# Sum of squares of the context norm: three additions on GpSimd and one product with ones, in place of eight products

## The reference

```
def rms_norm_2(x, w):
    x32 = x.astype(jnp.float32)
    y = x32 * lax.rsqrt(jnp.mean(x32 * x32, axis=-1, keepdims=True) + EPS)
    return (y * w.astype(jnp.float32)).astype(x.dtype)
...
    hc = modulate(rms_norm_2(xc, norm1_w[layer]), mc[0], mc[1])     # xc = ctx, 256 x 1024
        kc = split_heads(hc @ wi[:, K_OFF:V_OFF], RET_HEADS)
        vc = split_heads(hc @ wi[:, V_OFF:G_OFF], RET_HEADS)
```

## Time and profile before

| | us |
|---|---|
| median of 3 runs | 1617.76 |
| range of the runs | 1616.62 to 1618.76 |
| the profiled execution | 1616.73 |
| its span, first to last instruction | 1615.0 |

### The profile page before, as it was taken

How to read it: one execution, slowest core, us unless ns; L and a number is a source line. 1 busy time by engine, 2 the same in 40 slices (tenths; PEclk the granted TensorE clock), 3 DMA queues, 4 the chain that set the end, 5 groups by cost and what they waited for, 6 DMA issues and landing times.

```text
span 1615.0 us, 19990 instructions
## 1 busy us (share of the span) xinstructions
PE 1562.0 (97%) x7623; PEld 1262.7 (78%) x7623; DVE 898.0 (56%) x1114; ACT 773.8 (48%) x925; POOL 119.5 (7%) x95
## 2 busy tenths in 40 slices
PE   6999999999999899989899999999999999999998
PEld 5767777888787678868688888887886788888887
DVE  5434334345578788977553453544365655555565
ACT  6554445323557688856544333454134443443334
POOL 1101001000022233310010000000000000000000
PEclk9999999999989999999999999999999999999999
DMA  4457463224099999842412121222331323333221
GB/s 152 144 179 247 169 224 130 79 95 134 27 324 353 344 357 361 320 156 79 149 55 76 53 77 52 90 79 69 143 102 52 105 87 106 95 98 106 81 85 72
DMA packets 179857, 230.42 MB, mean 143 GB/s; under 512 B 12730, under 2 KB 151286, under 8 KB 176463
## 3 DMA queue, kind: packets, MB, share of 16 engines
q1 hardware_dynamic: 171712, 216.95, 39.6%
q0 software_dynamic: 7600, 12.41, 2.1%
q10 hardware_dynamic: 479, 0.16, 0.0%
HBM read 226.52 MB, written 18.37 MB: 152 GB/s over the span
## 4 chain that ended last, share of the span: by engine, by line
PE 84%; DVE 5%; ACT 4%; DMA 3%; issue 3%; ACTq 0%; POOL 0%; DVEq 0%; POOLq 0%
PE psum L459 21%; PE psum L461 20%; PE psum L460 20%; DMA hg<-h_rows,at_row 2%; PE psum L1885 2%; PE psum L1887 2%; PE psum L1886 2%; PE psum L775 1%; DMA y_rows<-y_sb,at_row 1%; PE psum L857 1%; ACT w_hi L432 1%; DVE pre L539 1%; PE psum L1912 1%; PE psum L1861 1%; PE psum L1913 1%
## 5 line engine op out<-in xcount | busy, mean ns | idle before, releaser
L459 PE MATMUL psum<-h_hi,w_hi 128*128 128x512 f32 x1160 | 462.6, 399 | 9.2 <-DVE w_lo L436 3.6
L460 PE MATMUL psum<-h_lo,w_hi 128*128 128x512 f32 x1160 | 453.2, 391 | 0.0
L461 PE MATMUL psum<-h_hi,w_lo 128*128 128x512 f32 x1160 | 453.1, 391 | 0.0
L436 DVE TENSOR_TENSOR w_lo<-raw,w_hi 128x2048 fp32r<-128x2048 f32 (+1 forms) x98 | 222.4, 2270 | 232.2 <-ACT w_hi L432 232.2
L459 PEld LDWEIGHTS psum<-h_hi,w_hi 128*128 128x128 f32 x1160 | 218.6, 188 | 68.5 <-issue 17.4
L461 PEld LDWEIGHTS psum<-h_hi,w_lo 128*128 128x128 f32 x1160 | 218.5, 188 | 46.7
L460 PEld LDWEIGHTS psum<-h_lo,w_hi 128*128 128x128 f32 x1160 | 218.9, 189 | 44.2 <-issue 1.4
L432 ACT ACTIVATE w_hi<-raw 128x2048 fp32r<-128x2048 f32 (+2 forms) x99 | 186.1, 1879 | 67.6 <-PE psum L461 64.5
L489 ACT ACTIVATE sq<-x 128x512 f32<-128x512 f32 x56 | 35.2, 631 | 142.3 <-DVE x L1379 81.7
L1833 DVE TENSOR_TENSOR w_lo_more<-raw_more,w_hi_more 128x2048 fp32r<-128x2048 f32 x34 | 77.8, 2287 | 23.3 <-ACT w_hi_more L1826 14.1
L1833 DVE TENSOR_TENSOR w_lo<-raw,w_hi 128x2048 fp32r<-128x2048 f32 x34 | 77.7, 2285 | 10.1 <-ACT w_hi L1826 7.2
(11 more groups left out here) (427 smaller groups left out, 2584.7 us busy)
## 6 DMA issues: line engine op xcount, KB each, us to landing
raw<-in_w_up SPq DMA_DIRECT2D x67, 512.0 KB
wm_raw<-in_w_mod SPq DMA_DIRECT2D x24, 1024.0 KB, 5.9
raw<-in_w_in SPq DMA_DIRECT2D x18, 1024.0 KB
raw<-in_w_in SPq DMA_DIRECT2D x33, 512.0 KB
raw_more<-in_w_down SPq DMA_DIRECT2D x24, 512.0 KB
raw<-in_w_gate SPq DMA_DIRECT2D x23, 512.0 KB
raw_more<-in_w_gate SPq DMA_DIRECT2D x22, 512.0 KB
raw_more<-in_w_up SPq DMA_DIRECT2D x22, 512.0 KB
```

The costliest lines, as they stand in the source:

```text
L436: dve.tensor_tensor(w_lo[j][:, 0:tiles, :], raw[j][:, 0:tiles, :], w_hi[j][:, 0:tiles, :].bitcast(F32), ALU.subtract).then_inc(G["lo_ready ...
L459: pe.matmul(to, w_hi[j][:, tile, :], hi_k, start=(k == 0), stop=False)
L460: pe.matmul(to, w_hi[j][:, tile, :], lo_k, start=False, stop=False)
L461: return pe.matmul(to, w_lo[j][:, tile, :], hi_k, start=False, stop=last)
```

## The change

Ahead of slot 1, TensorE takes one product with `ones` of chunk 0 of `ctx_sq` in place of eight, and waits for `L["ctx_sq"]` to reach 7 instead of 4. A new function `ple_gpsimd` stands between `moe_gpsimd` and `ret_gpsimd` on GpSimd: when the four squares are done, it adds chunks 4 to 7 to chunks 0 to 3 (1024 columns), then chunks 2 and 3 to 0 and 1 (512 columns), then chunk 1 to chunk 0 (256 columns). Each addition waits for the one before and adds 1 to `L["ctx_sq"]`.

```
@@ ple_tensor
-                    pe.wait_ge(L["ctx_sq"], 4)
-                    for k in range(KC):
-                        done = pe.matmul(psum[:, 6, 0:CTX], ones[:, :], ctx_sq[:, k, :], start=(k == 0),
-                                         stop=(k == KC - 1))
-                    done.then_inc(L["ctx_rstd"], 1)
+                    pe.wait_ge(L["ctx_sq"], 7)
+                    pe.matmul(psum[:, 6, 0:CTX], ones[:, :], ctx_sq[:, 0, :], start=True, stop=True)\
+                      .then_inc(L["ctx_rstd"], 1)
@@
+        def ple_gpsimd(pool):
+
+            pool.wait_ge(L["ctx_sq"], 4)
+            for n, half in enumerate((4, 2, 1)):
+                if n:
+                    pool.wait_ge(L["ctx_sq"], 4 + n)
+                pool.tensor_tensor(ctx_sq[:, 0:half, :], ctx_sq[:, 0:half, :], ctx_sq[:, half:2 * half, :], ALU.add)\
+                    .then_inc(L["ctx_sq"], 1)
@@ block.gpsimd
-            for stage in (start_gpsimd, mix_gpsimd, moe_gpsimd, ret_gpsimd):
+            for stage in (start_gpsimd, mix_gpsimd, moe_gpsimd, ple_gpsimd, ret_gpsimd):
```

## The result

| | before | after |
|---|---|---|
| median of 20 runs each, us | 1617.78 | 1620.32 |
| range, us | 1615.55 to 1620.81 | 1618.42 to 1623.17 |
| the profiled execution, us | 1616.73 | 1620.82 |
| its span, us | 1615.0 | 1619.1 |

The ratio after to before is 1.0016, with a 95% interval of 1.0009 to 1.0022: the medians differ by 2.5 us, less than the 0.2% that the prediction took as what can be told from no change, but its interval lies clear of 1.

A forecast was written before the change was run, and what follows sets the result against it. The chain on ScalarE and VectorE was taken to set slot 3, hiding TensorE's saving. GpSimd's additions would delay VectorE by 0.7 + 1.05 + 0.5 = 2.3 us, from 1617.76 to 1620.1 (1619.3 to 1621.0; wider range 1617.2 to 1622.2).

The forecast's parts named there:

- The products were worth nothing: TensorE ahead of slot 1: removing 14 of 16 matmul instructions saves 2.9 us there, worth nothing at the end.
- the cover: The chain on ScalarE and VectorE up to slot 3's w_lo, said to hide the 2.9 us saved on TensorE.
- GpSimd's own price: Three additions on GpSimd: 2.39, 1.29 and 0.74 us alone, the first beginning 0.08 us after ScalarE's end.
- The first term: VectorE's gains and slot 1's w_lo beside the first addition: w_lo 0.8 us late, 0.1 to spare, 0.7 reaches the chain.
- The second and third: Second and third additions take turns with VectorE's sig times pl and x plus sig: 1.05 and 0.5 us.
- The sum: The three delays on VectorE's chain make 2.3 us later at slot 3; forecast time 1620.1.
- TensorE is idle for 2.3 us: TensorE ahead of slot 3: slot 2 done at 757.9, 2.3 us before slot 3's new start at 760.2.
- Rival B: GpSimd waits out VectorE's four two-input instructions; TensorE sets slot 3, +2.6 us, lower clock up to 1.7: 1621.8; chance 0.25.
- Rivals A and C: A: no collision that matters, gain hidden, 1617.8, chance 0.16; C: chain not binding, slot 3 earlier, 1616.4, chance 0.05.

The follow-up runs named there:

- e1: Kernel before with one product of chunk 0 in place of eight, seven chunks left out, nothing on GpSimd; ratio 1.0005 (0.9992 to 1.0017).
- e7: e1 with nine idle products on TensorE between slot 2 and slot 3; ratio 1.0005 (0.9991 to 1.0020).
- e6: Kernel before with four of eight context chunks moved one round later and the eight products in one pass each (fp32r squares); ratio 0.9995 (0.9980 to 1.0010).
- e4: The change with only GpSimd's first addition (1024 columns) and four products behind it; ratio 1.0019 (1.0006 to 1.0031) to the kernel before.
- e8: The change with four of the context's eight chunks moved one round later; ratio 1.0005 (0.9991 to 1.0019) to the kernel before.
- e2: Kernel before with its eight products kept and the three GpSimd additions beside them, result unused; ratio 1.0026 (1.0017 to 1.0036).
- e3: Kernel before with one product of chunk 0, which waits for six GpSimd memsets in place of additions; ratio 0.9998 (0.9987 to 1.0008).
- e9: e1 with five idle products on TensorE between slot 2 and slot 3; ratio 0.9990 (0.9979 to 1.0002).
- e10: Kernel before with four of the context's eight chunks moved one round later, a repeat measurement; ratio 0.9997 (0.9984 to 1.0011).

## Why the prediction was right, point by point

**The products were worth nothing.** Held: e1 has the same 30.33 us to slot 3. What the text gave as the cover, the chain on ScalarE and VectorE, ends in the w_lo that the row of slot 3 names in every kernel with the chain whole, but for e7, whose idle products overran it. The text also said that with this cover gone the gain would be the full 2.9 us. e6 doesn't bear that out: the same two engines hold TensorE again ahead of the next stage, and of 2.3 us taken off TensorE the next norm saw nothing.

**GpSimd's own price.** The first addition was put at 2.39 us and took 2.40; the start behind ScalarE was put at 0.08 us and is 730.07 - 729.37 - 0.61 = 0.09. The 1.29 and 0.74 us of the other two can't be read alone, since both waited.

**The first term, 0.7 us.** In the change w_lo starts 732.57 - 730.11 = 2.46 us behind the first gain instruction, where it was 1.72: 0.74 us. e4 shows the same 0.74 alone. w_lo was put 0.8 us late with 0.1 us to spare; it is 0.74 late and nothing was to spare.

**The second and third, 1.05 and 0.5 us.** Sig times pl ended at 732.88 and should, with the 1.84 us of offset, end at 734.72; it ended at 736.51, 1.79 late, of which 1.05 is the second addition's. X plus sig of chunk 1 is 738.28 - 1.84 - 734.25 = 2.19 late, so the third cost 0.40. Put: 0.5. The engines took turns as the forecast had it: w_lo went ahead of the second addition, though the two rows begin 0.02 us apart with the addition's first, and from then on each waiter was next.

**The sum.** 2.3 us put, 2.21 in the trace, 2.5 in the medians, and 1620.1 against 1620.32 us. Part of this agreement is luck: the medians alone couldn't tell 1.5 from 3.5 us.

**TensorE.** Slot 1 was put at 736.0, which is 737.84 with the offset, and began at 737.81. Slot 2's end was put at 757.9, so 759.74, and came at 760.86. The 1.1 us between are the lower clock behind the wait, which over 736 to 742 has a mean of 0.72 (in e8, without it, slots 1 and 2 take 1.1 us less):

```profile
736.00:742.00 6.00, 4.85 (x15) 3.94 (x16) 4.46 (x7) 3.60 (x4) 1.05 (x1) 0.72 0.55 176
```

So the forecast's "TensorE is idle for 2.3 us" ahead of slot 3 became 1.05 us, and slot 3 ran at full clock. Rival B had the parts right (the clock falls, and ahead of slot 3 that costs up to 1.7 us: 1.5, 1.6 and 1.4 us in e1, e2 and e4) and their place in this kernel wrong: the long wait came earlier, the lower clock went into slot 1, and there VectorE's larger delay hid it. The forecast had put its price at nothing in the sum and left it to rival B; that the idle time ahead of slot 3 stayed at 1.05 us is a second piece of luck. Whether a lower clock reached slot 3 in others of the 20 runs of the change stays open; one was profiled.

**Rivals A and C** fall with the rows: w_lo of slot 1 did not start near its old place, and slot 3 began at VectorE's pace.

## What to carry to other kernels

Work taken off an engine that is 97% busy is worth only as much as what it waits for next allows, and here another chain of work held that, at slot 3 and again ahead of the next stage. Work given to an idle GpSimd isn't free if it reads SBUF while VectorE runs instructions with two SBUF inputs: look for the collision in the timeline, sum what each side waits, and see whether those instructions lie in the chain. And ask what an engine does with the time that it is given: a TensorE that idles for three microseconds ahead of the next block may pay 1.5 us more in clock, though it doesn't always.

## What the hardware showed beyond what was expected

Three instructions of 8 columns each on VectorE, 0.31 us in all, took 2.54 us beside a GpSimd addition of 2.40 us: how long they waited went by the addition and not by their own size. Six memsets on GpSimd, busy for 6.02 us, left the same instructions at 0.32 us.

A longer idle time of TensorE made the block behind it slower by 1.4 to 1.6 us through the granted clock. It did so in the three kernels whose rows name 2.8 to 3.4 us of idle time ahead of slot 3 (e1, e2, e4), and in none of the four with 0.2 to 1.1 us (before, after, e3, e9). But the same idle time can go either way. Besides the 3.25 us of the change and the 3.28 us of e8, there is a place that all twelve kernels share. Some 65 us behind the anchor, in the stage `ret`, TensorE waits 2.06 to 2.12 us for w_lo; it is the wait of the earlier trace rows. Over the 14 us from 62 us behind the anchor, the clock was 0.88 in eight of the profiles and 1.00 in four (e3, e6, e8, e10). What decides between the two is not shown here. 0.88 over 14 us is 1.7 us lost, nearly as much as the change's whole effect, so a profile of each kernel is compared stage by stage and not by its total.
